# State-space blocks: the first half of the tiles turned and scanned inside the recurrence's output product

## The reference, cut to what matters

```python
y_a = rwkv7_time_mix(z_mix, ...)          # ends with: return y @ w_proj
bu_re = jnp.einsum('gpc,bsgc->bsgp', bbar_re, uf)
bu_im = jnp.einsum('gpc,bsgc->bsgp', bbar_im, uf)
_, _, xr, xi = lax.associative_scan(_complex_scan_op, (a_seq_re, a_seq_im, bu_re, bu_im), axis=1)
y = (jnp.einsum('gcp,bsgp->bsgc', c_re, xr) - jnp.einsum('gcp,bsgp->bsgc', c_im, xi)
     + d_skip.reshape(G, C) * uf)
y = jax.nn.gelu(y.reshape(bsz, seq, SSM_WIDTH), approximate=False)
z = y @ w_glu + b_glu                     # za * sigmoid(zb) is y_b
x = x + (g_a * y_a + g_b * y_b) @ w_out[l]
```

## Time and profile before

| | |
|---|---|
| median of three runs | 2790.93 us |
| the profiled execution | 2791.15 us, its span 2789.4 us |
| TensorE products busy | 2683.7 us (96%) |
| VectorE busy | 1880.1 us (67%) |
| ScalarE busy | 1327.9 us (48%) |
| GpSimd busy | 267.2 us (10%) |
| mean granted TensorE clock | 0.988 of full speed |
| output product, tiles 2 to 7 | 1892.6 to 1925.4 us |
| state-space blocks | 1925.4 to 1975.7 us |

### The profile page before, as it was taken

One profiled execution on the slowest core, in us unless ns is written; L12 is line 12 of the kernel. 1 busy time (PEld: TensorE's weight loads), 2 busy tenths in 40 slices (PEclk: granted clock), 3 DMA queues, 4 the chain that ended last, 5 costly groups with the idle time before them and its releaser, 6 DMA issues. The chain is left out here.

```text
span 2789.4 us, 41619 instructions
## 1 busy us (share of the span) xinstructions
PE 2683.7 (96%) x16618; PEld 2106.1 (76%) x16618; DVE 1880.1 (67%) x2866; ACT 1327.9 (48%) x1941; POOL 267.2 (10%) x429
## 2 busy tenths in 40 slices
PE   7999999999999999999999989889899999999998
PEld 4756644777888888877778888767778878888886
DVE  7678987567666466784987716765656576656676
ACT  4147765468555434464441114452324655544344
POOL 0115630001000000000000002110000110000000
PEclk9999999999999999999999999999999999999999
DMA  7721100446566888731563341116243666677884
GB/s 271 225 77 39 50 1 1 144 146 238 208 230 224 304 273 290 259 132 49 144 163 122 140 139 67 72 64 197 95 139 122 221 213 230 233 288 256 296 285 151
DMA packets 206418, 474.00 MB, mean 170 GB/s; under 512 B 49072, under 2 KB 70192, under 8 KB 199920
## 3 DMA queue, kind: packets, MB, share of 16 engines
q1 hardware_dynamic: 188304, 393.73, 42.6%
q0 software_dynamic: 17920, 77.61, 7.1%
HBM read 344.09 MB, written 124.29 MB: 168 GB/s over the span
## 5 line engine op out<-in xcount | busy, mean ns | idle before, releaser
L2199 PE MATMUL psum<-merged_operand 128*128 128x512 f32 x1536 | 360.7, 390 | 0.0
L2199 PEld LDWEIGHTS psum<-merged_operand 128*128 128x128 f32 x1536 | 288.3, 188 | 60.7
L2199 PE MATMUL psum<-h_half_operand 128*128 128x512 f32 x1344 | 316.8, 391 | 0.0
L2199 PEld LDWEIGHTS psum<-h_half_operand 128*128 128x128 f32 x1344 | 252.2, 188 | 55.5 <-issue 1.0
L2199 PE MATMUL psum<-h_half_operand,weight_parts_operand 128*128 128x512 f32 x768 | 177.4, 392 | 0.8 <-DVE weight_parts_operand L2706 0.6
L2199 PEld LDWEIGHTS psum<-h_half_operand,weight_parts_operand 128*128 128x128 f32 x768 | 143.6, 188 | 34.0 <-DVE weight_parts_operand L2706 2.7
L3707 PE MATMUL psum<-x_operand,weight_high 128*128 128x512 f32 x448 | 140.6, 395 | 2.1 <-DVE z_mixed L3319 2.1
L3707 PE MATMUL psum<-o_operand,weight_high 128*128 128x512 f32 x448 | 138.4, 390 | 0.0
L3707 PE MATMUL psum<-x_operand,weight_low 128*128 128x512 f32 x448 | 138.0, 389 | 0.0
L2706 DVE TENSOR_TENSOR weight_parts_operand<-weight_ring,weight_parts_operand 128x1024 fp32r<-128x1024 f32 x66 | 80.7, 1223 | 84.2 <-ACT weight_parts_operand L2356 84.0
L2706 DVE TENSOR_TENSOR h_half_operand<-o,h_half_operand 128x1024 fp32r<-128x1024 f32 (+1 forms) x58 | 74.1, 1297 | 71.7 <-ACT h_half_operand L2491 50.9
(11 more groups left out here) (657 smaller groups left out, 5924.6 us busy)
## 6 DMA issues: line engine op xcount, KB each, us to landing
o<-in_w_ff SPq DMA_DIRECT2D x80, 512.0 KB, 4.6
merged<-hidden_terms SPq DMA_DIRECT2D x56, 512.0 KB, 5.9
hidden_upper<-in_w_ff_down SPq DMA_DIRECT2D x48, 512.0 KB, 4.8
weight_ring<-in_w_out SPq DMA_DIRECT2D x32, 512.0 KB, 3.4
hidden_terms<-weight_parts POOLq DMA_DIRECT2D x16, 1024.0 KB
hidden_terms<-weight_ring POOLq DMA_DIRECT2D x16, 1024.0 KB, 8.2
hidden_upper<-in_w_ff_up SPq DMA_DIRECT2D x32, 512.0 KB, 4.7
o<-hidden_terms SPq DMA_DIRECT2D x28, 512.0 KB, 6.2
```

The lines of the kernel that those rows point to most:

```text
L2199: mm = pe.matmul(bank, w[:, at:at + P], tiles(r, i), start=opens and m == 0, stop=closes and m == 2, skip_group_check=resumed)
```

## The change

The steps of a four are taken out of `ssm_blocks` into a new function, `ssm_steps`, whose parts both functions call.

- The TensorE turns u for four 0 behind tile 2, and for four 1 behind tile 3. It makes the state inputs of four 0 in the middle of tile 3 (before its third slice) and those of four 1 behind tile 4. The ScalarE's copies of u stand behind its copies of tiles 2 and 3.
- The VectorE turns the inputs of four 0 behind the gate of tile 2, scans behind tile 3, turns the states behind tile 4, turns the inputs of four 1 behind tile 5 and scans behind tile 6. The states of four 1 come behind the gate of tile 7.
- The SP loads u, win and table once y is split, before slabs 6 and 7 and before the lag loads.
- `g_a` has room for four gates and not eight. The gates of tiles 4 and 5 are loaded behind the lag loads, those of tiles 6 and 7 behind q and once tile 3 has been gated.
- The temporaries of the turning (`t`) have two parts and not four; the scan's output room serves for the other two, and the first product of a state is written into the state's place and completed there. The states lie in columns of the weight ring that narrow slabs leave free. `y_by_token` is placed so that it meets the rooms of the gates, and the first copy of outputs waits for the last gate.

```diff
+    turn_banks, state_banks = (4, 4, 6, 4), (6, 4, 0, 2)
...
+    def turn_u(pe, four):
+        if four == 0:
+            pe.wait_ge(u_landed, 16)
+        elif four == 1:
+            pe.wait_ge(u_copied, 2)
+        else:
+            pe.wait_ge(K.dve_done.sem, at["turned", four - 2])
+        for g in range(2):
+            for i in range(4):
+                mm = pe.transpose(psum[:, turn_banks[four] + g, i * P:(i + 1) * P], u[:, 2 * (4 * four + i) + g, :],
...
+    def state_inputs(pe, four):
+        if four == 0:
+            pe.wait_ge(win_landed, 16)
+        pe.wait_ge(u_copied, 2 * four + 2)
...
+    def turn_inputs(c, four):
+        dve = c.eng
+        tiles = slice(4 * four, 4 * four + 4)
+        er, ei = table[:, 0, tiles, :], table[:, 1, tiles, :]
+        if four == 0:
+            dve.wait_ge(table_landed.sem, table_at)
+        else:
+            c.wait(at["states", four - 1, 1])
+        dve.wait_ge(v_ready, four + 1)
+        v_re, v_im = (by_tile(psum[:, state_banks[four] + o, :]) for o in range(2))
+        for out, v, e in ((t[:, 0], v_re, er), (run[:, 0], v_im, ei), (t[:, 1], v_im, er), (run[:, 1], v_re, ei)):
+            c.step(dve.tensor_tensor(out=out, in0=v, in1=e, op=ALU.mult))
+        at["turned", four] = c.n
+        for o, op in ((0, ALU.add), (1, ALU.subtract)):
+            c.wait(at["turned", four] - 2 + 2 * o)
+            c.step(dve.tensor_tensor(out=t[:, o], in0=t[:, o], in1=run[:, o], op=op))
...
+    def turn_states(c, four):
+        dve = c.eng
+        tiles = slice(4 * four, 4 * four + 4)
+        e_re, e_im = (table[:, o, tiles, 0:P - 1] for o in range(2))
+        r_re, r_im = (run[:, o, :, 0:P - 1] for o in range(2))
+        x_re, x_im = (x[:, four % 2, o, :, 1:P] for o in range(2))
+        c.wait()
+        if four >= 2:
+            dve.wait_ge(out_ready, 2 * (four - 1))
+        for out, r, e in ((x_re, r_re, e_re), (t[:, 0, :, 1:P], r_im, e_im), (x_im, r_re, e_im), (t[:, 1, :, 1:P], r_im, e_re)):
+            c.step(dve.tensor_tensor(out=out, in0=r, in1=e, op=ALU.mult))
+        for o, (out, op) in enumerate(((x_re, ALU.subtract), (x_im, ALU.add))):
+            c.wait(c.n - 2 + o)
+            c.step(dve.tensor_tensor(out=out, in0=out, in1=t[:, o, :, 1:P], op=op))
+            at["states", four, o] = c.n
...
-    LOADS, BY_ACT = 2 + 2 * B, 2
+    LOADS, BY_ACT, GATES = 2 * B, 2, 4
...
             def _(sp):
-                sp.wait_ge(squared, NT)
-                for half in range(2):
-                    tiles = slice(4 * half, 4 * half + 4)
-                    sp.dma_start(g_a[:, tiles, :], gate_dram[tiles].rearrange("t p s -> p t s")).then_inc(landed[half].sem, 16)
-                for n in range(RING, N):
+                def load_gates(t, many, f):
+                    sp.dma_start(g_a[:, t % GATES:t % GATES + many, :], gate_dram[t:t + many].rearrange("t p s -> p t s")) \
+                        .then_inc(f.sem, 16)
+
+                def load_slab(n):
                     sp.wait_ge(K.slab_split.sem, split0 + n - RING + 1)
                     sp.dma_start(K.ring[:, n % RING, 0:WT * P], weights[n]).then_inc(K.slab_loaded[n % RING].sem, 16)
+
+                sp.wait_ge(squared, NT)
+                load_gates(0, GATES, landed[0])
+                load_slab(RING)
+                load_slab(RING + 1)
+                sp.wait_ge(K.tile_split.sem, tile0 + 2 * WT)
+                sp.dma_start(y[:].rearrange("p t s -> p (t s)"), u_dram).then_inc(ssm["u_landed"], 16)
+                sp.dma_start(win_t, win_dram.rearrange("p o n (s f) -> p o (n s) f", f=P)).then_inc(ssm["win_landed"], 16)
+                sp.dma_start(table, table_dram).then_inc(landed[2].sem, 16)
+                for n in range(RING + 2, N):
+                    load_slab(n)
                 sp.wait_ge(K.pool_done.sem, pool0 + 1)
                 lag = lag_dram.rearrange("p g n (s f) -> p g (n s) f", f=P)
                 for m in range(B):
                     for g in range(2):
                         sp.dma_start(toeplitz[16 * m:16 * m + 16, g, :, (B - 1 - m) * 16:], lag[:, g, :, 0:(m + 1) * 16]) \
                             .then_inc(K.load_done.sem, 16)
-                sp.dma_start(win_t, win_dram.rearrange("p o n (s f) -> p o (n s) f", f=P)).then_inc(K.load_done.sem, 16)
-                sp.wait_ge(K.tile_split.sem, tile0 + 2 * WT)
-                sp.dma_start(y[:].rearrange("p t s -> p (t s)"), u_dram).then_inc(K.load_done.sem, 16)
-                sp.dma_start(table, table_dram).then_inc(landed[2].sem, 16)
+                sp.wait_ge(K.posted.sem, gated0 + 2)
+                load_gates(GATES, 2, landed[1])
                 sp.dma_start(q, q_dram).then_inc(landed[3].sem, 16)
+                sp.wait_ge(K.posted.sem, gated0 + 4)
+                load_gates(GATES + 2, 2, last_gates)
                 prefetch(sp, K, after, K.slab_used.n, N)
...
+                        if n == 3 and k == 2:
+                            ssm["state_inputs"](pe, 0)
...
                     mm.then_inc(K.slab_used.sem, 1)
+                    if n == 2:
+                        ssm["turn_u"](pe, 0)
+                    elif n == 3:
+                        ssm["turn_u"](pe, 1)
+                    elif n == 4:
+                        ssm["state_inputs"](pe, 1)
...
+                    if n in (2, 3):
+                        ssm["copy_u"](act, n - 2)
...
+                c = Chain(dve, K.dve_done)
+                ssm["first_block"](c)
                 for n in range(N):
                     if n + 2 < N:
                         split_w(n + 2)
-                    dve.wait_ge(landed[n // 4].sem, landed0[n // 4] + 16)
+                    if n < GATES + 2:
+                        dve.wait_ge(landed[n // GATES].sem, landed0[n // GATES] + 16)
+                    else:
+                        dve.wait_ge(last_gates.sem, 16)
                     dve.wait_ge(K.acc_free.sem, free0 + n + 1)
-                    dve.tensor_tensor(out=out[:, n, :], in0=out[:, n, :], in1=g_a[:, n, :], op=ALU.mult) \
+                    dve.tensor_tensor(out=out[:, n, :], in0=out[:, n, :], in1=g_a[:, n % GATES, :], op=ALU.mult) \
                         .then_inc(K.posted.sem, 1)
+                    if n == 2:
+                        ssm["turn_inputs"](c, 0)
+                    elif n == 3:
+                        ssm["scan"](c, 0)
+                    elif n == 4:
+                        ssm["turn_states"](c, 0)
+                    elif n == 5:
+                        ssm["turn_inputs"](c, 1)
+                    elif n == 6:
+                        ssm["scan"](c, 1)
+                K.dve_done.n = c.n
...
+                ssm["turn_states"](c, 1)
+                for four in range(EARLY_QUADS, QUADS):
+                    ssm["turn_inputs"](c, four)
+                    ssm["scan"](c, four)
+                    ssm["turn_states"](c, four)
...
+                turn_u(pe, 2)
+                turn_u(pe, 3)
+                pe.wait_ge(K.acc_free.sem, K.acc_free.n + 2)
+                state_inputs(pe, 2)
                 pe.wait_ge(K.load_done.sem, K.load_done.n)
-                turn_u(0)
-                turn_u(1)
-                pe.wait_ge(K.acc_free.sem, K.acc_free.n + 2)
-                state_inputs(0)
-                turn_u(2)
-                state_inputs(1)
-                turn_u(3)
-                state_inputs(2)
                 add_inputs(0)
                 add_states(0)
...
+                    if four == 0:
+                        act.wait_ge(K.posted.sem, K.posted.n + 2)
...
+                u_early = K.sbuf(rw, "u_by_block", [P, 2, M // 2, P])
+                turned, run = (K.sbuf(rw, name, [P, 2, 4, P]) for name in ("turned_inputs", "scanned"))
+                states = K.ring[:, :, WT * P:2 * WT * P].rearrange("p (b o) (s f) -> p b o s f", b=2, s=4)
+                u_place, u_rows = [u_early], y[:].rearrange("p t (n f) -> p (t n) f", f=P)
+                ssm = ssm_steps(nc, K, s5, u_rows, (u_place, turned, run, states))
                 with ExitStack() as inner:
                     first_half = K.pair(inner, "y_first_half", [P, WT, HALF])
-                    g_a = K.sbuf(inner, "g_a", [P, KT, S])
+                    g_a = K.sbuf(inner, "g_a", [P, 4, S])
```

144 lines of the change are left out of this document (62 added, 82 removed).

## The result

The changed kernel takes 2775.78 us, the median of four runs (2774.46 to 2778.22). The kernel before took 2792.09 us beside it (four runs, 2789.29 to 2796.63). The ratio is 0.9950 with a 95% interval of 0.9937 to 0.9963: between 10 and 18 us faster. A repeat in five rounds gave 2776.96 us and 0.9953 (0.9939 to 0.9966), beside 2789.97 us for the kernel before. So the two medians of the first comparison lie 16.3 us apart and those of the repeat 13.0. The forecast was 2781.9 us, with a range of 2778.5 to 2787.5: right in its sign, too small in its size.

The account below looks back on a forecast made before the run. The bound was taken to be one VectorE chain in the state-space blocks, behind a product leaving it 20 us spare. Last state 7.7 us earlier plus 1.6 of clock made 9.3: 2791.15 to 2781.9 us, range 2778.5 to 2787.5.

Parts of the forecast that it names:

- gates 4 and 5 landed, gate 4 starts: Load behind the lag loads: lands at 1922.45 us (1921.4 to 1923.8), ending a 7.3 us VectorE wait.
- TensorE's stall before tile 7: In the output product: the TensorE stands from 1925.8 to 1928.5 us for the split of slab 7.
- last state made: End of the VectorE's chain: the last state comes at 1962.6 us where it was 1970.26, 7.7 us earlier.
- last use of states: TensorE's final product with states: 2.79 us at full clock where it took 4.39 at 0.61.
- gain of the stretch: From the end of tile 2 to the end of the last use of states: 7.7 + 1.6 = 9.3 us.
- lag price: Time the 16 lag loads add behind slab 7, ahead of gates 4 and 5: 13.5 us (12.4 to 14.8).
- VectorE's list: VectorE steps summed from gate 4 at 1922.45 us to the last state at 1962.6, with 0.5 of hand-over.
- 26.6 us from tile 7 to the last use: TensorE work behind tile 7: ready at 1960.5 us, then still waiting about 1.5 us for the VectorE.
- early gates: Rival: gates 4 and 5 land by about 1915 us, TensorE limits, end 13.4 us earlier at 2777.8; chance 0.12.
- clock term: Last use of states on the TensorE: full clock after a shorter wait, 4.39 - 2.79 = 1.6 us earlier.
- Slow loads: Rival: loads in the new place are slower by 2 to 6 us, giving 2784 to 2788 us; chance 0.15.
- rival on the other side: Lag loads at twice their price delay gate 4, states 0 and split 7: slower than before, 2795.4 us; chance 0.05.

Follow-up runs that it names:

- gates first: Changed kernel with the gates of tiles 4 and 5 loaded ahead of the lag loads: 2779.10 us, ratio 0.9958 against the kernel before.
- third kept-busy kernel: Kernel before with 7, 15 and 15 idle TensorE products ahead of the last three uses of states: 2787.68 us, ratio 0.9990.
- late gates: Changed kernel with the gates of tiles 4 and 5 loaded behind q: 2783.34 us, ratio 0.9975; run again for its profile, 2783.62 us.

## Why the prediction was too small

The mechanism was right, and so were most steps. In times of the kernel before (the changed kernel's less 1.35 us):

| step | forecast | measured |
|---|---|---|
| table landed, inputs 0 start | 1905.3 | 1904.6 |
| gates 4 and 5 landed, gate 4 starts | 1922.45 | 1920.1 |
| TensorE's stall before tile 7 | 2.7 us | about 0.2 us |
| tile 7 ends | 1933.9 | 1931.7 |
| last state made | 1962.6 | 1959.1 |
| last use of states | 2.79 us, full clock | 2.82 us, full clock |
| gain of the stretch | 9.3 us | 12.8 us |

**The lag price was too high: 2.3 of the 3.5 us.** This is the step that failed: the prediction added the lag loads, 13.5 us and at least 12.4, whole behind the landing of slab 7. Counted from the issue of u (1887.58), slab 7 landed after 20.4 us, as forecast. The last lag load came 1919.0 - 1908.0 = 11.0 us later, below my lower end, and the gates 2.5 behind it, as forecast: 33.9 us in place of 36.35. (Tile 2 ended 0.1 sooner after the issue of u than before, so 2.3 of the 2.45 remain in the ruler.) The gate of the repeat came after 33.55 us, so the shorter price is not luck.

What the price left out is an overlap, as far as the rows go. In the kernel before, the last slab landed at about 1897.4 (2.7 us after its issue), and the last lag load followed 13.3 us later:

```profile
state_space<-s_lag SPq DMA_DIRECT2D x1, 128.0 KB, 8.2
```

It was issued at 1902.5 and landed at 1910.7. So 13.5 was right for that place, where no small packet had moved before 1896.5. In the changed kernel the small packets set in at about 1905 (43 had moved by 1905 and 1122 by 1906), beside the end of the table and the slabs, and the last of the loads landed at 1919.0. Both times this takes some 14 us, but 0.9 us of it lay ahead of the last slab's landing in the old place and some 3 us in the new one. Both ends of the prediction's range came from the old place, so the range could not hold this. No run separates the overlap from a quicker transfer, and without 14 of the 16 loads the gates came 8.1 us sooner, which fits either.

**The VectorE's list was too long: 1.2 us.** From the gate of tile 4 to the last state I had summed 40.15 us. It took 1960.42 - 1921.48 = 38.94. I had added durations of single rows, and consecutive instructions of the VectorE start closer than their durations: the gate lasts 1.23 us, and the next instruction starts 1.14 later; the split starts 1.06 and not 1.15 before its successor; before a gate the scans take 2.54 and not 2.66; and the hand-over between fours 1 and 2 was 0.03 (1940.47 to 1940.50) and not 0.5. The hand-over is the largest piece; the rest is 0.11 us or less at each of the other steps. The shared buffers cost nothing, as priced: a four still takes 1950.48 - 1940.50 = 9.98 us.

**The TensorE was nearer than the sum showed.** Its 26.6 us from tile 7 to the last use were right (26.86 with a wait of 0.35). The prediction left it 1.5 us of slack and 9.3 of gain; the full gain to the TensorE's own limit was 13.4, and the changed kernel got 12.8 of it. The rival "early gates" had this limit right (13.36 with the gates first). Its condition was too strict: it said that gates by 1915 were needed, and 12.8 us came with gates at 1920.1. The wait for gates was on the path, as forecast, but the forecast chain and the limit were only 4.1 us apart. A gate that comes 2.3 us sooner and a list that is 1.2 shorter take up 3.5 of that, and the stall before tile 7 goes from 2.7 us to 0.2 with them.

**The clock term was right**, 1.6 us, and the third kept-busy kernel has it alone, 1.57. Its reason was half right. The prediction argued with the length of the last wait, and the waits of 1.9 to 2.4 us come out either way. It held because the waits shrank to 0.35 us, where every profile has the full clock.

**The range was too narrow.** It was made of terms and rivals worked out from one profile, without the scatter between executions. (The forecast's own range, 2780.5 to 2783, is 0.2 to 0.3 us off its terms of -1.1 and +1.3, which give 2780.8 to 2783.2; nothing hangs on it.) The kernel before ran from 2784 to 2797 us in the comparisons, and four runs of a kernel have a median that moves by a microsecond or two; in the profiles alone L2144 and the phase of the first tiles make 1.6 and 1.5 us each. The repeat's 2776.96 lies 1.5 us outside the range; the first result, 2775.78, is 2.7 outside. With the mechanism's 12.8 us the sum would have been 2791.15 - 12.8 = 2778.4, itself 0.1 below the range. What lies between that and the two medians, 1.4 to 2.6 us, no stage accounts for, and it is of the size of the scatter.

**The other rivals.** Slow loads did not come: u landed at 1896.1 and the table at 1905.9, so win and table, 2 MB each, took 9.85 us together, which is 426 GB/s. By the 358 GB/s that the Trainium skill states (DMA: Bandwidth & Descriptors, "Where 436 GB/s comes from") they would, as an estimate, have taken 11.7 us; this trace again does not agree. The rival on the other side, a gate so late that the kernel becomes slower, names a real mechanism: gates 5.3 us later cost 7.4 us from the issue of u, through the stall at slab 7 and the clock behind it. That such a kernel ends up slower than before was not seen: at 2783.34 us the ratio was still 0.9975.

## What to carry to other kernels

When work moves under another stage, first find the limit of the next engine (here the TensorE from tile 7 on) and forecast the gain as the smaller of the two, with the distance between them as part of the range. Sum a list of instructions by start-to-start distances, not by durations. Price a batch of small loads by its landing and not by its issue, and see whether it runs beside the load ahead of it before adding its time behind. Put nothing that another engine waits for (here the split of slab 7) behind a late load in an engine's list: in the profile with late gates the end moved by 7.4 us for a gate 5.3 us later.
